# The beginning of a two-block kernel: residual and modulation loaded first, squares summed on VectorE, h made from a rooted residual, two units multiplied a tile at a time

## The reference, cut to what matters

```
ada = c @ w_ada + b_ada                      # 6 vectors of 1024: sh1, sc1, gt1, sh2, sc2, gt2
h = rms_norm(x, norm1_w) * (1 + sc1) + sh1   # x is 512 x 1024
proj = h @ w_in                              # attention, RWKV and gate columns
```

## Time and profile before

| | us |
|---|---|
| median of 3 runs | 2491.84 (2487.38 to 2496.64) |
| the profiled execution | 2490.61 |
| its span in the profile | 2489.2 |
| TensorE busy | 2347.4 (94%) |

### The profile page before, as it was taken

One profiled execution on the slowest core, in us unless ns is written; L12 is line 12 of the kernel. 1 busy time (PEld: TensorE's weight loads), 2 busy tenths in 40 slices (PEclk: granted clock), 3 DMA queues, 4 the chain that ended last, 5 costly groups with the idle time before them and its releaser, 6 DMA issues.

```text
span 2489.2 us, 33880 instructions
## 1 busy us (share of the span) xinstructions
PE 2347.4 (94%) x14398; PEld 1851.1 (74%) x14398; DVE 1424.4 (57%) x1790; ACT 685.3 (28%) x853; POOL 889.0 (36%) x419
## 2 busy tenths in 40 slices
PE   5999999899998799989999988999999999999998
PEld 2777776566666588768888866888888887888887
DVE  3113223577767410666665559788863457888733
ACT  3122112443433322232222221322222332322212
POOL 3422221111110244444444433444444444444442
PEclk8999999899999799979999999999999999999999
DMA  6433332212120333323333313233333322333331
GB/s 216 127 102 111 106 98 78 64 37 51 44 46 10 93 103 99 91 60 102 93 106 101 91 55 102 80 99 102 93 110 94 93 86 84 100 95 96 110 95 56
DMA packets 412039, 222.57 MB, mean 89 GB/s; under 512 B 33823, under 2 KB 409458, under 8 KB 410610
## 3 DMA queue, kind: packets, MB, share of 16 engines
q1 hardware_dynamic: 387394, 208.28, 29.0%
q10 hardware_dynamic: 24496, 12.13, 1.8%
HBM read 214.61 MB, written 5.77 MB: 89 GB/s over the span
## 4 chain that ended last, share of the span: by engine, by line
PE 59%; DVE 6%; issue 0%; ACT 0%; POOL 0%; DVEq 0%; ACTq 0%
PE bank L309 59%; DVE ev_s L2321 0%; PE bank L312 0%; DVE h_low L1929 0%; DVE mg_r_low L1907 0%; DVE g_c L2131 0%; DVE x_res L2278 0%; DVE sq L512 0%; DVE ev_z L2288 0%; DVE sq L508 0%; DVE ev_s L2319 0%; DVE sq L2028 0%; DVE ev_s L2292 0%; DVE ev_low L2333 0%; DVE ev_s L2324 0%
## 5 line engine op out<-in xcount | busy, mean ns | idle before, releaser
L305 POOL TENSOR_TENSOR w_low<-w_raw,w_high 128x1024 fp32r<-128x1024 f32 (+1 forms) x331 | 850.7, 2571 | 1473.1 <-ACT w_high L298 1473.1
L309 PE MATMUL bank<-h_high,w_high 128*128 128x512 f32 x2008 | 809.8, 403 | 38.4 <-DVE h_low L519 20.6
L309 PE MATMUL bank<-h_low,w_high 128*128 128x512 f32 x2008 | 788.9, 393 | 0.0
L298 ACT CAST w_high<-w_raw 128x1024 fp32r<-128x1024 f32 (+1 forms) x331 | 358.5, 1084 | 917.3 <-PE bank L309 899.4
L309 PE MATMUL bank<-h_high,w_low 128*128 128x512 f32 x2008 | 512.5, 395 | 0.0
L309 PEld LDWEIGHTS bank<-h_high,w_high 128*128 128x128 f32 x2008 | 380.2, 189 | 147.4 <-issue 32.9
L309 PEld LDWEIGHTS bank<-h_high,w_low 128*128 128x128 f32 x2008 | 378.7, 190 | 85.0 <-issue 4.6
L309 PEld LDWEIGHTS bank<-h_low,w_high 128*128 128x128 f32 x2008 | 381.1, 190 | 78.1 <-issue 3.4
L309 PE MATMUL bank<-g_high,w_high 128*128 128x512 f32 x352 | 137.9, 392 | 2.3 <-ACT g_c L2110 2.3
L309 PE MATMUL bank<-g_low,w_high 128*128 128x512 f32 x352 | 137.8, 391 | 0.0
L2007 DVE TENSOR_TENSOR x_res<-bank,x_res 128x512 f32<-128x512 f32 x32 | 22.1, 692 | 169.2 <-PE bank L309 169.2
(11 more groups left out here) (368 smaller groups left out, 2888.9 us busy)
## 6 DMA issues: line engine op xcount, KB each, us to landing
w_raw<-in_w_in SPq DMA_DIRECT2D x58, 512.0 KB, 4.6
w_raw<-in_w_up SPq DMA_DIRECT2D x44, 512.0 KB, 3.8
w_raw<-in_w_ffn_gate SPq DMA_DIRECT2D x44, 512.0 KB, 3.8
w_raw<-in_w_ffn_up SPq DMA_DIRECT2D x44, 512.0 KB, 3.8
w_raw<-in_w_ffn_down SPq DMA_DIRECT2D x32, 704.0 KB, 4.4
w_raw<-in_w_ada SPq DMA_DIRECT2D x32, 512.0 KB, 3.8
w_raw<-in_w_down SPq DMA_DIRECT2D x16, 704.0 KB, 4.5
w_raw<-in_w_in ACTq DMA_DIRECT2D x21, 512.0 KB, 4.3
```

Source lines behind the costliest of these rows:

```text
L298: self.A.copy(self.w_high[:, u % SPLIT_SLOTS, 0:k * P], self.raw_of(key)[:, 0:k * P]).then_inc(*self.S.rounded(*key))
L305: self.G.tensor_tensor(self.w_low[:, slot, 0:k * P], self.raw_of(key)[:, 0:k * P], self.w_high[:, slot, 0:k * P].bitcast(F32), ALU.subtrac ...
L309: return self.T.matmul(out, lhsT, rhs, start=start, stop=stop, skip_group_check=True)
```

## The change

- **SP queue.** `x`, the eight parts of `w_ada` and the first four unit weights are issued before any vector. Vector groups 1 to 5 follow behind them. Group 0 (norm weights, `b_ada`, `c`: six transfers) is issued from ScalarE's queue.
- **TensorE.** Turns group 0 alone, then `x`; three of the eight parts of `c @ w_ada`; one product of ones with the summed squares (`sum_pe`); the other five parts; the columns, those of the gain first. Then units 0 and 1 together: for each k, high and low of both; then the 8 + 8 matmuls with the low weights. The five other vector blocks are turned after the nine units of pair 0 (`vectors_pe`).
- **ScalarE** squares a tile as soon as it is there, loads the table for ln ahead by a dummy, copies its lines, rounds units 0 and 1, then makes the high tiles of h itself from the rooted tile with scale and bias.
- **VectorE** adds the squares into `rinv` (eight additions), makes x times the inverse root for all k (`rooted`, eight products into the room of `x_rows`), then its lines and columns, then per k one instruction for the tile of h and one for the rest, for odd k too.
- **GpSimd** makes the rests of units 0 and 1 before it waits for the columns, and no rest of h.

```diff
 def setup_sp(self):
     Y.dma_start(self.xrow[:], ...)
+    for k in range(DT):
+        Y.dma_start(self.ada_w[:, k, :], w_ada[:, k, 0:2 * D])
+    for r in range(RAW_SLOTS):
+        self.load_raw(r, Y)
     Y.wait_ge(*S_.pool_setup.at("rows"))
-    for g, group in enumerate(VECTORS):
-        ...
-    self.ada_sp()
+    for g in range(1, len(VECTORS)):
+        self.load_vectors(g, Y, S_.vectors_loaded)
+def begin_pe(self):
+    T.wait_ge(*S_.first_loaded.at(0))
+    self.turn(self.bank[1][:, 0:P], self.rows[:, 0, :])
+    T.wait_ge(*S_.x_loaded.at("x"))
+    for f in range(DT):
+        b = 2 + f % 4
+        self.empty(b)
+        for t in range(4):
+            self.turn(self.bank[b][:, t * P:(t + 1) * P], self.xrow[:, t, f * P:(f + 1) * P])
+    T.wait_ge(*S_.dve_setup.at("vec", 0))
+    for k in range(DT):
+        if k == 3:
+            self.sum_pe("norm1", S_.dve_norm.at("norm1", "squares"))
+        self.ada_rows_pe(k)
+    self.ada_columns_pe()
+    for k in range(DT):
+        T.wait_ge(*S_.h_low_even.at("norm1", k))
+        for u, key in enumerate(units):
+            ...
+            self.mm(out, tile(self.w_high, u, k), self.h_high[:, k, :], k == 0, False)
+            self.mm(out, tile(self.w_high, u, k), self.h_low[:, k, :], False, False)
+    for u, key in enumerate(units):
+        T.wait_ge(*S_.lowered.at(*key))
+        for k in range(DT):
+            self.mm(self.bank[6 + u][:], tile(self.w_low, u, k), self.h_high[:, k, :], False, k == DT - 1)
+def begin_act(self):
+    A.wait_ge(*S_.pool_setup.at("rows"))
+    self.load_vectors(0, A, S_.first_loaded)
+    for f in range(DT):
+        if f % 2 == 0:
+            A.copy(self.x[:, f, :], self.bank[2 + f % 4][:])
+        if f >= 2:
+            A.wait_ge(*S_.dve_norm.at("norm1", "added", f - 2))
+        A.activation(self.sq[:, f % 2, :], self.x[:, f, :], ACT.Square)
+    A.activation(self.spare[:], self.ones[:, 0:1], ACT.Ln)
+    self.root_act("norm1")
+    A.wait_ge(*S_.ada_row.at("rows"))
+    ...
+    self.round_unit(("qkv", 0, 0))
+    self.round_unit(("qkv", 0, 1))
+    for k in range(DT):
+        A.activation(self.h_high[:, k, :], self.rooted(k), ACT.Identity, bias=..., scale=...)
+def begin_dve(self):
+    V.tensor_copy(self.vec[:, 0:P], self.bank[1][:, 0:P])
+    for f in range(DT):
+        if f % 2:
+            V.tensor_copy(self.x[:, f, :], self.bank[2 + f % 4][:])
+        V.wait_ge(*S_.act_norm.at("norm1", "square", f))
+        V.tensor_tensor(self.rinv[:], self.rinv[:], self.sq[:, f % 2, :], ALU.add)
+    self.sum_dve("norm1")
+    for k in range(DT):
+        V.tensor_tensor(self.rooted(k), self.x[:, k, :], self.rinv[:], ALU.mult)
+    ...
+    for k in range(DT):
+        V.scalar_tensor_tensor(self.sq[:, k % 2, :], self.rooted(k), self.gain1[:, k:k + 1],
+                               self.grid(self.mod, k, (0, S)), ALU.mult, ALU.add)
+        if k:
+            self.begin_low(k - 1)
+    self.begin_low(DT - 1)
+def vectors_pe(self):
+    for g in range(1, len(VECTORS)):
+        ...
+        self.turn(self.bank[b][:, ...], self.rows[:, g, :])
+def vectors_dve(self):
+    for b in range(2):
+        V.tensor_copy(self.vec[:, ...], self.bank[b][:, ...])
+    self.rwkv_vectors()
```

More of the change, by code:

```diff
@@ L408, in setup_sp, with load_vectors @@
-        S_.vectors_loaded.table["all"] = S_.vectors_loaded.value
-        self.ada_sp()
[L411 to L415, removed]
+        for g in range(1, len(VECTORS)):
+            self.load_vectors(g, Y, S_.vectors_loaded)
+    def load_vectors(self, g, queue, signal):
+        row = 0
+        for name, n in VECTORS[g]:
+            last = name == VECTORS[g][-1][0]
+            if name == "mu_low":
+                m = self.io["mu_shift"]
+                for r, c in enumerate((3 * D, 3 * D + P, RWKV_IN - P)):
+                    queue.dma_start(self.rows[row + r:row + r + 1, g, :], m[0:1, c:c + P]).then_inc(
+                        *signal(*((g,) if last and r == 2 else ())))
+            else:
+                queue.dma_start(self.rows[row:row + n, g, :], self.vector_source(name)).then_inc(*signal(*((g,) if last else ())))
+            row += n
@@ L428, in setup_pe @@
             ins.then_inc(*S_.turned("x", f))
[L429 to L435, removed]
-    def setup_dve(self):
+            self.emptied[b] = (S_.dve_setup if f % 2 else S_.act_setup, ("x", f))
+        T.wait_ge(*S_.dve_setup.at("vec", 0))
+        for k in range(DT):
+            if k == 3:
+                self.sum_pe("norm1", S_.dve_norm.at("norm1", "squares"))
+                self.emptied[7] = (S_.dve_norm, ("norm1", "mean"))
+            self.ada_rows_pe(k)
@@ new lines, in begin_pe @@
+        self.ada_columns_pe()
+        self.end("pe", "ada")
+        units = [("qkv", 0, 0), ("qkv", 0, 1)]
+        tile = lambda t, u, k: t[:, u, k * P:(k + 1) * P]
+        for k in range(DT):
+            T.wait_ge(*S_.h_low_even.at("norm1", k))
+            for u, key in enumerate(units):
+                if k == 0:
+                    T.wait_ge(*S_.rounded.at(*key))
+                    self.empty(6 + u)
+                out = self.bank[6 + u][:]
+                self.mm(out, tile(self.w_high, u, k), self.h_high[:, k, :], k == 0, False)
+                self.mm(out, tile(self.w_high, u, k), self.h_low[:, k, :], False, False)
@@ L446, in setup_dve @@
-        self.end("dve", "setup")
+            last = min(4 * b + 3, len(VECTORS) - 1)
+            first = 4 * b if b else 1
+            V.wait_ge(*S_.turned.at("vec", last))
+            V.tensor_copy(self.vec[:, first * P:(last + 1) * P], self.bank[b][:, first % 4 * P:(last % 4 + 1) * P]
+                          ).then_inc(*S_.dve_setup("vec", 4 * b + 3))
+        V.wait_ge(*self.own("dve"))
+        self.rwkv_vectors()
     def rms_act(self, name, src, made, tiles=DT):
```

191 lines of the change are left out of this document (100 added, 91 removed).

## The result

| | before | after |
|---|---|---|
| median of the runs, us | 2490.64 (2487.38 to 2496.64, 4 runs) | 2471.98 (2470.49 to 2473.55, 4 runs) |
| profiled execution, us | 2490.61 | 2470.49 |
| its span | 2489.2 | 2469.3 |
| VectorE copies unit 1 | 72.05 | 56.55 |
| VectorE's first reduction of scores | 111.66 | 97.42 |

The table already splits the miss, as far as one profile of each kernel can. The beginning, measured up to the first reduction of scores behind the vector blocks, gave 111.66 - 97.42 = 14.2 instead of 11.5; and the later part, the same work in both kernels, took 5.6 less where the prediction had it unchanged.

The account below looks back on a forecast made before the run. TensorE, busy 94% of the span, was taken as the bound, with time to win only before VectorE copies unit 1 (72.05 us). A gain of 13.0 there less 1.5 later made 11.5 us: 2480 us, range 2474 to 2488.

Parts of the forecast that it names:

- the finish line: VectorE's copy of unit 1 out of PSUM, 72.05 us; time won there, less later costs, is the change's worth.
- Part 2: Squares, ScalarE and VectorE alternating: summed at 25.0, slower (14.8 for 12.8) but starting 6.5 earlier; root at 30.0.
- Part 1: Transfers: w_ada behind x lands near 28.3, 6.9 us earlier; group 0 at about 6; x turned at 9.1.
- Part 3: Modulation on TensorE: lines ready at 32 with the half clock, otherwise 30.2, before VectorE asks for them.
- Parts 4 and 5: VectorE's rooted products 5.6, lines 1.40, columns 2.1; GpSimd's rests of units 0 and 1 add 2.6; first h tile 41.7.
- Part 6: Tiles of h: 1.49 us each instead of 2.4, last rest at 54.0; unit 1 at 59.0 against 72.0, gain 13.0.
- Part 7: Later cost: vector blocks turned near 97 us and a wait before the first scores, 1.5 us, bounds 0.8 and 3.
- B: Rival: GpSimd's rests delay nothing and the clock stays up; first tile at 39.1, gain 14.1, 2477.7 us; chance 0.18.
- A: Main case: everything as summed, 2480 us; chance 0.50.
- C: Rival: TensorE stays at half clock through units 0 and 1, unit 1 at 65.9, 2487.2 us; chance 0.14.
- D: Rival: VectorE's chain longer, every handover 0.1 more and both GpSimd rests in full, 2484.5 us; chance 0.13.
- E: Rival: group 0's vectors land only with w_ada (28.3), delaying the turns of x, 2499.5 us; chance 0.05.

Follow-up runs that it names:

- e12: Kernel before with VectorE adding up the squares and one product of ones on TensorE instead of eight: 2487.14 us, ratio 0.9981.
- e9: Kernel after with GpSimd filling the block of ones 75 times, which delays the beginning: 2487.83 us, ratio 0.9979.
- e2: Kernel after with all vectors back on SP's queue ahead of w_ada: 2475.75 us, ratio 0.9939.
- e8: Kernel after with VectorE's copies of x ahead of its additions of squares: 2469.13 us, ratio 0.9906.
- e17: Kernel after with VectorE's copies of x ahead of its additions, run once more: 2469.65 us, ratio 0.9909.
- e10: Kernel after with VectorE's copies ahead of its additions and the gain read from PSUM: 2471.11 us, ratio 0.9916.
- e6: Kernel after with unit 0 done wholly before unit 1 instead of paired: 2476.20 us, ratio 0.9938.
- e7: Kernel after with tiles of h made as before (no rooted pass, odd rests on GpSimd): 2475.24 us, ratio 0.9931.
- e4: Kernel before with w_ada issued right behind x and all 28 vectors from ScalarE's queue: 2506.98 us, ratio 1.0059.
- e15: Kernel after with seven unread products of ones and a single column on TensorE ahead of the sum of squares: 2471.95 us, ratio 0.9919.
- e16: Kernel after with forty unread products of ones and a single column on TensorE ahead of the sum of squares: 2483.99 us, ratio 0.9966.

## Why the prediction was wrong, step by step

Two things failed. **The first is the premise of the finish line**, "because all later stages shift along with it". They shift, but not unchanged: 4.5 to 5 of the 19 us lie behind the first reduction of scores (18.7 - 14.2 in the result, 19.8 - 14.9 over all runs). By e12 they go with Part 2, where the squares leave TensorE, and by e9 at least 2.5 of them are independent of the starting moment. The prediction costed that part at its own place only and put its effect on all that follows at nothing. Without it the time would have been 2476 to 2477, inside the range. None of its signs of being wrong could catch this, since all look at the first 60 us; and there none of them came.

**The second is the size of the beginning**, 14.2 to 15.4 in three profiles for 11.5 summed. Up to the copy of unit 1, 56.55 for 59.0, the terms missed by (us, minus is earlier): start of the turns +0.5, squares -1.5, product, mean and root +0.5, rooted tiles -0.6, from the lines to the first tile -0.6, tiles of h -0.8, the end +0.1.
- *Part 1.* x was turned at 9.56 for 9.1 (x took 8.6 us to land, not 8.0; in e2, with `w_ada` behind the vectors, 8.1), so 0.5 was lost. `w_ada` landed 1.2 later than summed, which cost nothing; half of that is a slip of the sum, since 8 + 20.9 is 28.9 and not 28.3. e2 shows what its order is worth, 5 to 6 at unit 1.
- *Part 2.* Added up at 23.99 for 25.0: the 0.5 put on for delay by shared memory did not come, and a pair of tiles took 3.12 (VectorE's additions start at 11.94, 15.06 and 18.18) for 3.39. The product of ones took 2.08 at the half clock, mean and root as summed: 29.45 for 30.0. e8 and e17 show that the alternation itself cost 3 to 4 us here, of which 0.9 to 2.6 reach unit 1.
- *Part 3.* As summed: the lines were never late. One reading was off: TensorE did not idle from 38 to 42 in the kernel before, it turned lines into columns (1.99 us from 39.85), busy 2.38 of these 4 us when the half clock came.
- *Part 4, rooted tiles.* Eight of them took 4.91, not 5.6: each lasts 0.69, but starts 0.60 after the one before.
- *Parts 4 and 5, columns and GpSimd.* Summed were 2.1 for the columns and 2.6 for GpSimd's rests, 4.7 from lines to tile; it took 4.06. The place was right: one gain stood 1.65 beside GpSimd's 5.46 us. But the two don't add: by e10 the columns alone, at the half clock (4.50 us on TensorE, against 1.05 + 1.99 before), take the 4.06, and the hold lies within. First tile of h at 39.90 for 41.7. The Trainium skill (SBUF — State Buffer, Who interferes with whom) lets an instruction with one operand in PSUM go through; in e10 the gain from PSUM took 0.16 beside GpSimd, and the trace agrees.
- *Part 6.* 1.39 a tile for 1.49, since a tile's two instructions overlap by 0.04 where a handover of 0.05 was put on (ScalarE took 0.80 for a high tile, not 0.63, and still ran ahead); the last rest at 51.43 for 54.0, and 5.1 from there to unit 1's copy for 5.0. e6 and e7 show the two halves of the gain: 3.5 to 4.6 for the pairing, 4.1 to 5.2 for the tiles.
- *Part 7.* The vector blocks: units 1 to 8 and the blocks took 97.42 - 56.55 = 40.87 where before has 39.61, so 1.26 for 1.5. Of TensorE's gap of 1 to 2 us before the first scores, 0.53 came.

Parts 2, 4, 5 and 6 erred in one direction, 0.6 to 1.5 us each: durations of instructions by themselves were added up where they overlap in a row, handovers and a delay were put on top, and two waits that lie beside each other were summed. The rivals: B came nearest in the number, and that is luck: its gain of 14.1 is what the beginning gave, but the clock was at half and one rest did hit the gain, and its time of 2477.7 is still 5.7 above the measured one. A was right in its mechanisms up to the first scores and small in its terms. C did not come: full clock at 48. D did not come. E did not come: group 0, last issued at 3.78, was there at some 9, 5 us later in place of the 2.0 taken, which is just before x. A row of TensorE in e8, whose transfers are those of the kernel after:
```profile
9.07 0.45 PE L312 MATMUL bank<-ident,vec_rows 128*128 128x128 f32 x1 [9.07 <-DMA vec_rows<-in_c]
```
But e4 shows that small transfers do come late beside the bulk; here they were few enough (160 packets) to be hidden by x.

**What stays open.** Why 4.6 to 10 us of such products near the start go with 5 to 8 us more of half clock over the following 2.4 ms, and why seven small products (1.72 us) do not, was not found; the place of TensorE's instructions alone is ruled out by e15, the starting moment as the whole of it by e9. e16, with 13.6 us of small products, has the dearer later part (2376.2, 118 us at half clock); it mixes its activity with a longer beginning and other pauses and settles neither.

## What to carry to other kernels

Compare the part of the trace that the change doesn't touch as well, in several profiles of each kernel and against the mean clock of all runs: here a quarter of the gain lay there, and a delayed copy of the new kernel and one edit put into the old one told it from chance. Where instructions of one shape follow each other, take the duration from a group of such (eight in 4.91), not from one that stands alone. Put small transfers that gate the start ahead of bulk ones, or count their packets: beside the bulk, the second queue moved some 37 packets a microsecond here, so 160 were through by 9 us and 882 only by 30.

## What was unexpected of the hardware

- Vectors issued on ScalarE's queue by 13.5 were complete only at 31.18 (e4): 181 to 204 of their packets passed in 5 us beside SP's, with some 400 GB/s in all. In the kernel before, where they go ahead of `w_ada`, the last one took 2.0 us.
- The same kernel is granted a different clock from run to run: 0.972 to 0.975 for the kernel after, with 2468.92 to 2474.8 us. Work that TensorE does near the start shifts the time of all of the rest (e12: 4.6 us by one edit).
- TensorE pauses for 0.4 to 1.8 us in places that move with its number of instructions, each time until 1.2 to 1.7 us after a packet of the DMA queue "instruction" has landed.
